# Four weight buffers, one Newton root per pair, and work moved between engines in a three-block kernel

## The chip, the cores and the metric

One Trainium2 chip, one of its cores. The metric is device time in microseconds (us) of one execution, lower is better. The chip's engines are named as in the profile: PE is TensorE (PEld its weight loads), DVE is VectorE, ACT is ScalarE, POOL is GpSimd, SP is the sync engine, which here issues all DMAs.

## What is computed

Three transformer blocks, one after the other, over one sequence of 256 tokens with 2048 channels, all in fp32.

```python
x = first_block(x, ...)    # RMS norm; w_in; RWKV-7 mixing beside banded attention,
                           # each gated by silu; two branch products, merged by sigmoid gates;
                           # w_out; x + rms_norm(o)
x = second_block(x, ...)   # RMS norm; w_in; sparse attention beside spatial gating:
                           #   vn = layer_norm(gelu(v))
                           #   mixed = einsum('gts,bcsgd->bctgd', tril(w_s), vn) + b_s
                           #   out = gelu(u) * mixed
                           # gates, w_out, squared-relu feed-forward, RMS norm
return third_block(x, ...) # pooling beside dilated attention, feed-forward, RMS norm
```

RWKV needs per head 1/max(|kk|, 1e-12) and, after its scan, 1/sqrt(var + 64e-5); every RMS norm needs 1/sqrt(mean of squares).

## The kernel before, in words

Activations lie channels on partitions: a chunk is 128 channels by 256 tokens. All large products are one stream over weights (sections `qkv` to `down3_1`, lines 196 to 218, 256 output columns per block). A unit is 1024 rows by 256 columns (1 MB), loaded by SP into `ring` (RING = 4 units). A slot is half a unit, 512 rows; there are 1084 slots. For each slot ScalarE copies the weights to their rounded high half (`split_high`, L2205) and VectorE makes the low half (`split_low`, L2212) in `w_parts` (PARTS = 3 slots). TensorE then runs eight products of 512 columns with the high half (L2282) and eight of 256 with the low half (L2288), and raises `slot_used`. When a block ends, ScalarE copies one half of the result out of PSUM (L1845), VectorE adds the other (L1932), and scaling, activation or residual follow in phases 1 to 3, some on GpSimd (L1895).

Each engine walks the slots q in the same order. In its iteration q ScalarE makes the high half of slot q + 2, and VectorE the low half. A load of unit u waits until unit u - RING is split:

```python
            if u >= RING:
                sp.wait_ge(low_split, 2 * (u - RING) + 2)
...
            if q >= PARTS:
                act.wait_ge(slot_used, q - PARTS + 1)
```

All other work runs beside the stream as threads (class `Beside`, L59): a thread has a start slot and a pace, each of its programs yields ticks, and a tick runs at place start + tick x pace, at q, q + 0.34 or q + 0.67 of that engine's walk. So the order on each engine is fixed when the kernel is built; semaphores do the rest, and a thread's step that waits holds the stream's work behind it on that engine. The start thread begins at -1 with pace 1.34.

What the change touches:

- **Start** (L306 to L444). SP loads x in two halves, then units 0 and 1. TensorE transposes x (L384), VectorE copies it out (L424) and ScalarE and VectorE split it (L409, L461). ScalarE squares whole rows after copy groups 3 and 7 (L414). VectorE makes the root, TensorE spreads it over partitions (L400), which gives `rstd`.
- **InverseRoot** (L77). A Newton root on VectorE, eleven small dependent operations (L89 to L94).
- **Rms** (L465). Squares of a block's output on ScalarE (L492, L495), added up on GpSimd into `acc` (L504) except the last, then summed over partitions on TensorE (L516): first `acc`, then the last squares, both behind the wait for the last squares.
- **Rwkv** (L812). Two threads, each four head pairs i; their side products are issued at L1026. Per i and thread VectorE copies the norm (L907), runs a root and a clamp (L911), then makes the sigmoid (L915), for which TensorE waits; and another root after the variance (L969).
- **Gates and branch.** The gates go out to `gate_scratch` in DRAM (L2001) and come back in 16 loads (L2045). The branch section has two slots a block, blocks alternating RWKV and attention, their operands split at L577 and L585 by `y_split`, then `ya_split`. Gate and branch are merged at L1954 to L1959.
- **post** (L2059 to L2110), between blocks 1 and 2 (stages out and index2): sums, root, spread, then VectorE scales o (L2071), adds x (L2075) and makes low halves (L2080); ScalarE makes high halves (L2108) and squares for `norm1`, and GpSimd adds two of those (L504).
- **Spatial gating** (L1403 to L1552), in sections ga2 and gb2. TensorE sums v over channels by 16 products with ones (L1443) and its squares by 32 (L1453). For each of 16 groups (class `Gating`, two threads, 7 ticks of 0.6 slots) TensorE transposes (L1542, L1543), ScalarE copies (L1528), VectorE masks the weights (L1516), TensorE adds the bias as a product with a row of ones (L1549) and the mixed product (L1550), and VectorE multiplies by u (L1522).

## Time and profile before

| | |
|---|---|
| median of 3 runs | 3639.61 us (3635.76 to 3640.41) |
| the profiled execution, own time | 3641.87 us |
| its span | 3640.1 us, 53150 instructions |
| PE busy | 3492.9 us (96%) |
| DVE busy | 2225.8 us (61%) |
| ACT busy | 1581.7 us (43%) |
| POOL busy | 276.9 us (8%) |
| DMA | 591.44 MB, mean 162 GB/s |
| mean granted TensorE clock | 0.977 of full |

Busy time of TensorE is the union of its matmuls; they are pipelined and their ends are modelled, so a row's duration can reach into the next one. One fp32 matmul in the code is two records in the trace outside the main stream. An idle time in brackets names what ended it. The page also has the span in 40 slices:

```profile
PEclk9999999989998999999999999999999999999999
DMA  6554332323653554544566556665545466566653
```

### The profile page before, as it was taken

The page shows a single profiled execution, that of the slowest core. Times are in us where ns is not written, and L with a number is a line of the kernel's source. Part 1 is how long each engine was busy: PE and PEld are TensorE (multiplying, and loading weights), DVE is VectorE, ACT ScalarE, POOL GpSimd, SP SyncE. Part 2 cuts the span into 40 slices and gives each one's busy share as a digit, 9 for nine tenths or more (in the row PEclk, how much of TensorE's full clock was granted, in tenths as well). Part 3 has the DMA queues.
Part 4 walks back from the last instruction along what each step waited for, and adds up shares of the span by engine and source line. Part 5 has one row for each costly group of instructions (what it writes and reads, how often), then busy time and mean ns, then how long its engine had stood idle before and what let it go on. Part 6 is the DMA issues. An engine that isn't in the chain of part 4 may idle for free.

```text
span 3640.1 us, 53150 instructions
## 1 busy us (share of the span) xinstructions
PE 3492.9 (96%) x22326; PEld 3009.5 (83%) x22326; DVE 2225.8 (61%) x3130; ACT 1581.7 (43%) x2140; POOL 276.9 (8%) x313
## 2 busy tenths in 40 slices
PE   7999999988998999999999999999999899999998
PEld 6887777767886887887888888888888788888887
DVE  5556654555746667665676546655677766456644
ACT  3444333333453445443544434444454444434444
POOL 2100122220010110000000000001000000000000
PEclk9999999989998999999999999999999999999999
DMA  6554332323653554544566556665545466566653
GB/s 187 172 176 146 116 119 91 97 90 106 219 180 88 185 174 151 174 139 139 185 183 188 185 186 184 189 193 185 175 151 161 150 187 191 188 186 186 187 183 127
DMA packets 587351, 591.44 MB, mean 162 GB/s; under 512 B 20886, under 2 KB 581350, under 8 KB 587111
## 3 DMA queue, kind: packets, MB, share of 16 engines
q1 hardware_dynamic: 587112, 588.04, 51.9%
q8 instruction: 176, 2.88, 0.3%
q14 instruction: 63, 0.52, 0.0%
HBM read 581.68 MB, written 6.32 MB: 162 GB/s over the span
## 4 chain that ended last, share of the span: by engine, by line
PE 86%; DVE 8%; ACT 3%; issue 2%; DMA 1%; SPq 0%; POOL 0%; ACTq 0%; DVEq 0%
PE gp L2282 50%; PE gp L2288 27%; PE sidep L1026 4%; DVE w_parts L2212 2%; ACT w_parts L2205 1%; PE sidep L516 1%; ACT lo_half L1845 0%; PE sidep L1549 0%; PE sidep L1550 0%; DMA high<-bias_rows 0%; DVE stage L1932 0%; DVE stage L1936 0%; DVE smalls L94 0%; DVE smalls L92 0%; PE sidep L1320 0%
## 5 line engine op out<-in xcount | busy, mean ns | idle before, releaser
L2212 DVE TENSOR_TENSOR w_parts<-ring,w_parts 128x1024 fp32r<-128x1024 f32 x1084 | 1375.0, 1277 | 917.5 <-ACT w_parts L2205 916.4
L2205 ACT ACTIVATE w_parts<-ring 128x1024 fp32r<-128x1024 f32 x1084 | 1134.2, 1056 | 1100.0 <-PE gp L2288 1040.9
L2282 PE MATMUL gp<-x_parts,w_parts 128*128 128x512 f32 x5856 | 1534.7, 402 | 28.4 <-issue 12.7
L2282 PEld LDWEIGHTS gp<-x_parts,w_parts 128*128 128x128 f32 x5856 | 1065.2, 192 | 230.9 <-issue 30.8
L2288 PEld LDWEIGHTS gp<-x_parts,w_parts 128*128 128x128 f32 x5856 | 802.3, 192 | 63.5 <-DVE w_parts L2212 5.7
L2288 PE MATMUL gp<-x_parts,w_parts 128*128 128x256 f32 x5856 | 837.5, 286 | 3.7 <-DVE w_parts L2212 3.7
L2282 PE MATMUL gp<-ff_parts,w_parts 128*128 128x512 f32 x2816 | 715.9, 396 | 4.8 <-ACT w_parts L2205 4.8
L2282 PEld LDWEIGHTS gp<-ff_parts,w_parts 128*128 128x128 f32 x2816 | 505.1, 188 | 101.8 <-ACT w_parts L2205 5.6
L2288 PEld LDWEIGHTS gp<-ff_parts,w_parts 128*128 128x128 f32 x2816 | 385.3, 188 | 32.0
L2288 PE MATMUL gp<-ff_parts,w_parts 128*128 128x256 f32 x2816 | 394.9, 282 | 0.0
L1845 ACT ACTIVATE lo_half<-gp 128x512 f32<-128x512 f32 x255 | 152.2, 597 | 479.6 <-PE gp L2288 479.4
L1932 DVE TENSOR_TENSOR stage<-gp,lo_half 128x512 f32<-128x512 f32 x184 | 127.1, 691 | 208.7 <-ACT lo_half L1845 208.6
L504 POOL TENSOR_TENSOR low<-low 128x512 f32<-128x512 f32 (+1 forms) x44 | 65.0, 1483 | 1971.6 <-ACT low L492 1319.3
L1861 ACT ACTIVATE ff_parts<-stage 128x512 fp32r<-128x512 f32 x64 | 40.5, 633 | 170.5 <-DVE stage L1967 170.5
L1026 PEld LDWEIGHTS sidep<-high 64*64 64x64 f32 x1760 | 68.4, 136 | 45.0 <-issue 18.8
L1026 PE MATMUL sidep<-high 64*64 64x64 f32 (+1 forms) x1760 | 81.9, 230 | 17.7 <-ACT high L1008 5.3
L1895 POOL TENSOR_TENSOR high<-high,rstd 128x512 f32<-128x512 f32 x40 | 56.3, 1408 | 517.0 <-DVE high L1932 517.0
L1932 DVE TENSOR_TENSOR high<-gp,lo_half 128x512 f32<-128x512 f32 x63 | 43.5, 691 | 62.2 <-ACT lo_half L1845 62.2
L1895 POOL TENSOR_TENSOR stage<-stage,rstd 128x512 f32<-128x512 f32 x32 | 43.7, 1365 | 411.3 <-DVE stage L1932 411.3
L1992 DVE TENSOR_TENSOR ff_parts<-stage,ff_parts 128x512 fp32r<-128x512 f32 x64 | 44.3, 692 | 49.1 <-ACT ff_parts L1861 49.1
L1936 DVE TENSOR_TENSOR stage<-stage,rstd 128x512 f32<-128x512 f32 x88 | 60.3, 685 | 0.2
L1967 DVE SCALAR_TENSOR_TENSOR stage<-stage 128x512 f32<-128x512 f32 x64 | 44.3, 692 | 2.2
(372 smaller groups left out, 1751.9 us busy)
## 6 DMA issues: line engine op xcount, KB each, us to landing
ring<-w_in SPq DMA_DIRECT2D x220, 1024.0 KB, 5.2
ring<-w_ff SPq DMA_DIRECT2D x128, 1024.0 KB, 5.6
ring<-w_up SPq DMA_DIRECT2D x64, 1024.0 KB, 5.8
ring<-w_down SPq DMA_DIRECT2D x64, 1024.0 KB, 5.5
ring<-w_out SPq DMA_DIRECT2D x48, 1024.0 KB, 5.5
ring<-w_branch_rwkv SPq DMA_DIRECT2D x8, 1024.0 KB, 5.5
ring<-w_branch_attn SPq DMA_DIRECT2D x8, 1024.0 KB, 5.4
gate_scratch<-stage SPq DMA_DIRECT2D x16, 256.0 KB, 2.3
```

The costliest lines, as they stand in the source:

```text
L504: m = pool.tensor_tensor(self.acc[k], self.acc[k], self.sq[b - 1][k], ALU.add)
L1026: return pe.matmul(out, lhs, rhs, start=start, stop=stop, skip_group_check=True)
L1845: act.activation(lo_half[:, k % 2], gp[:, k % 2, :, 1, :], ACT.Copy).then_inc(lo_copied, 1)
L1895: pool.tensor_tensor(to, to, over(rstd, 2), ALU.mult).then_inc(scaled_by_pool, 1)
L1932: v.tensor_tensor(to, gp[:, k % 2, :, 0, :], lo_half[:, k % 2], ALU.add).then_inc(block_evacuated, 1)
L1936: v.tensor_tensor(to, to, over(scaled_by[s.name], 2), ALU.mult).then_inc(scaled_by_vector, 1)
L1967: v.scalar_tensor_tensor(st, st, 0.0, st, ALU.max, ALU.mult).then_inc(finished_up, 1)
L1992: v.tensor_tensor(ff_parts[:, 2 * b:2 * b + 2, 1, :], st, ff_parts[:, 2 * b:2 * b + 2, 0, :].bitcast(F32), ALU.subtract).then_inc(ff_split, 1)
L2205: act.activation(w_parts[:, q % PARTS, 0], ring[:, u % RING, SLOT * (q % 2):SLOT * (q % 2) + SLOT, :], ACT.Copy).then_inc(high_split, 1)
L2212: v.tensor_tensor(w_parts[:, q % PARTS, 1], ring[:, u % RING, SLOT * (q % 2):SLOT * (q % 2) + SLOT, :], w_parts[:, q % PARTS, 0].bitcast(F ...
L2282: pe.matmul(gp[:, k % 2, j, :, :], w_parts[:, q % PARTS, 0, c, j * P:(j + 1) * P], operand(s, b, SLOT * n + c), start=(n == 0 and c == 0), ...
L2288: m = pe.matmul(gp[:, k % 2, j, 0, :], w_parts[:, q % PARTS, 1, c, j * P:(j + 1) * P], operand(s, b, SLOT * n + c)[:, 0, :], start=False, ...
```

## The change

It has these parts.

1. `w_parts` has four slots and `ring` three units. The sizes are equal, so the memory used stays the same. The order of the walks is not changed.
2. Start: unit 0 is loaded ahead of the second half of x; high and low half of slot 0 are made within the copy loop; the squares of whole rows move behind it, to tick 1 (place 0.34). The spread on TensorE moves to tick 1.25 (place 0.675), the parameter transposes to 1.5, VectorE's steps accordingly. SP loads unit 1 before the parameters and unit 2 after them, which is now all of the ring.
3. `Rms`: with three or more blocks, the `acc` half of the sums no longer waits for the last squares.
4. RWKV: thread 1 runs one root for both threads, over eight columns, after both have copied; likewise after the variance. TensorE's spreads wait for it.
5. Branch blocks alternate attention first; `ya_split` comes ahead of `y_split`, and the gate loads wait for `ya_split` as before.
6. post: the first group of four chunks is scaled and added in two halves, and its low halves come directly after; GpSimd's adds for `norm1` wait for all splits (`x_split`).
7. Gating: VectorE adds up v (two adds of 128x1024, one of their sum, one of 128x512) and the squares likewise (three of 128x1024 and one of 128x512); TensorE does 2 products instead of 16, and 4 instead of 32. The bias is loaded onto all partitions and added by VectorE before the product with u; the 32 bias products go.

The diff, cut to its core:

```diff
-RING = 4
-PARTS = 3
+RING = 3
+PARTS = 4
...
             for n in range(2):
+                if n:
+                    load_unit(sp, 0)
                 for t in range(2):
                     sp.dma_start(xrow[:, t, n * 1024:(n + 1) * 1024],
...
-            yield 1
+            yield 1.25
             pe.wait_ge(copied, 9)
             spread(pe, 1, 2, 1).then_inc(n_spread, 1)
...
-                if g in (3, 7):
-                    act.wait_ge(x_loaded[0], 32)
-                    act.wait_ge(x_loaded[1], 32)
-                    act.activation(row_squares, xrow[:, g // 4, :], ACT.Square,
-                                   accum_out=sums[:, g // 4:g // 4 + 1]).then_inc(rows_squared, 1)
+                if g == 3:
+                    split_high(act, 0)
+            yield 1
+            act.wait_ge(x_loaded[0], 32)
+            act.wait_ge(x_loaded[1], 32)
+            for t in range(2):
+                if t:
+                    act.wait_ge(rows_squared, 1)
+                act.activation(row_squares, xrow[:, t, :], ACT.Square, accum_out=sums[:, t:t + 1]).then_inc(rows_squared, 1)
...
+                if g == 4:
+                    split_low(v, 0)
-            yield 0.5
+            yield 1
             v.wait_ge(rows_squared, 2)
...
                 for part in (self.acc, self.sq[-1]):
-                    pe.wait_ge(self.squared, self.blocks)
+                    if part is not self.acc or self.blocks < 3:
+                        pe.wait_ge(self.squared, self.blocks)
...
                     dv.did(v.tensor_scalar(self.nrm, y[:, 0:4], 1e-30, None, ALU.max), "norm_copied")
-                    dv.wait(v, "norm_copied", i)
-                    dv.did(self.root.run(v, self.nrm, self.inv, self.half, self.part), "norm_rooted")
-                    dv.wait(v, "norm_rooted", i)
-                    dv.did(v.tensor_scalar(self.inv, self.inv, 1e12, None, ALU.min), "norm_inverted")
+                    if self.th == 1:
+                        for rw in rwkv:
+                            rw.dv.wait(v, "norm_copied", i)
+                        rwkv_roots.did(rwkv_root.run(v, *rwkv_eight), "norm_rooted")
+                        rwkv_roots.wait(v, "norm_rooted", i)
+                        rwkv_roots.did(v.tensor_scalar(rwkv_eight[1], rwkv_eight[1], 1e12, None, ALU.min), "norm_inverted")
...
-            sp.dma_start(bs[0:1], I["sgu_b_2"]).then_inc(sgu_loaded, 16)
+            sp.dma_start(bs, bass.AP(I["sgu_b_2"].tensor, 0, [[0, P], [P, 16], [1, P]])).then_inc(sgu_loaded, 16)
...
+            yield 4
+            pe.wait_ge(sgu_added, 4)
+            for c in range(2):
+                m = pe.matmul(sp_[:, 0, 0:TOK], ones[:, :], sgu_sq[:, 0, c, :], start=(c == 0), stop=(c == 1), skip_group_check=True)
+            m.then_inc(sgu_summed, 1)
+            yield 16
+            pe.wait_ge(sgu_added, 8)
+            for t in range(2):
+                for c in range(2):
+                    m = pe.matmul(sp_[:, 1, t:t + 1], sgu_sq[:, 0, c, t * P:(t + 1) * P], ones[:, 0:1],
+                                  start=(c == 0 and t == 0), stop=(c == 1), skip_group_check=True)
+            m.then_inc(sgu_summed2, 1)
...
-                    dv.did(v.tensor_tensor(u, self.y[:, 0:TOK], u, ALU.mult), "out")
+                    dv.did(v.tensor_tensor(self.vn.rearrange("p (t s) -> p t s", t=2), self.y[:, 0:TOK].rearrange("p (t s) -> p t s", t=2),
+                                           bs[:, g:g + 1, :].to_broadcast([P, 2, P]), ALU.add), "biased")
+                    dv.wait(v, "biased", i)
+                    dv.did(v.tensor_tensor(u, self.vn, u, ALU.mult), "out")
...
-                        pe.matmul(self.y[:, t * P:(t + 1) * P], ones[0:1, :], bs[0:1, g, :], start=True, stop=False, skip_group_check=True)
                         m = pe.matmul(self.y[:, t * P:(t + 1) * P], self.tok[:, t, :], self.tok[:, 2, :],
-                                      start=False, stop=True, skip_group_check=True)
+                                      start=True, stop=True, skip_group_check=True)
...
+        ya_split = Split(q1, 8, att_ready, S["zr"].end).thread("y_a", at("branch"))
         y_split = Split(v_, 0, y_ready, S["zr"].end).thread("y_r", at("branch"))
-        ya_split = Split(q1, 8, att_ready, S["zr"].end).thread("y_a", at("branch"))
...
-            scale(0)
-            add(0)
+            for n in range(2):
+                v.tensor_tensor(o1[:, 2 * n:2 * n + 2, :], o1[:, 2 * n:2 * n + 2, :], over(sp_[:, 1], 2), ALU.mult).then_inc(first_scaled, 1)
+                v.wait_ge(first_scaled, n + 1)
+                v.tensor_tensor(xt[:, 2 * n:2 * n + 2, :], xt[:, 2 * n:2 * n + 2, :], o1[:, 2 * n:2 * n + 2, :], ALU.add).then_inc(first_stored, 1)
+            low_halves(0)
             scale(1)
             add(1)
-            low_halves(0)
             scale(2)
...
         def post_pool(pool):
             yield 1.0
+            pool.wait_ge(x_split, norm1_xs0 + 4)
             norm1.add(pool, 1)
             norm1.add(pool, 2)
```

## Rows read from the trace of the kernel before

**Rows 1.** The page: the engine line, and one line of its DMA issues.

```profile
PE 3492.9 (96%) x22326; PEld 3009.5 (83%) x22326; DVE 2225.8 (61%) x3130; ACT 1581.7 (43%) x2140; POOL 276.9 (8%) x313
...
ring<-w_in SPq DMA_DIRECT2D x220, 1024.0 KB, 5.2
```

**Rows 2.** Stretches: stage down2_0, then ga2; busy (records), clock, DMA share, GB/s.

```profile
2029.99:2210.89 180.90, 180.90 (x1026) 157.50 (x1025) 90.13 (x82) 72.35 (x73) 0.00 (x0) 1.00 0.60 188
1524.36:1645.08 120.72, 120.72 (x709) 103.95 (x708) 73.97 (x101) 50.09 (x64) 11.19 (x8) 1.00 0.49 149
```

**Rows 3.** Groups of instructions by line: busy us, mean ns, idle before and its releaser.

```profile
L1549 PE MATMUL sidep<-high,ones 1*128 1x128 f32 x64 | 16.1, 332 | 4.7 <-DVE low L1516 4.7
...
L1443 PE MATMUL sidep<-high,ones 128*128 128x256 f32 x32 | 7.6, 379 | 0.0
...
L1453 PE MATMUL sidep<-ones,low 128*128 128x1 f32 x64 | 7.5, 246 | 0.0
...
L1478 DVE TENSOR_TENSOR high<-high,variance 128x1024 f32<-128x1024 f32 x4 | 4.9, 1220 | 0.0
```

**Rows 4.** Instructions in order of time, TensorE, in ga2: start, us, what.

```profile
1600.55 0.48 PE L1549 MATMUL sidep<-high,ones 1*128 1x128 f32 x2
1600.96 0.49 PE L1550 MATMUL sidep<-low 128*128 128x128 f32 x2
```

**Rows 5.** Order of time in the gates stage, third pair of RWKV heads; idle in brackets.

```profile
658.10 0.15 DVE L907 TENSOR_SCALAR smalls<-sidep 128x4 f32<-128x4 f32 x1
...
660.54 0.49 DVE L915 TENSOR_SCALAR high<-high 128x256 f32<-128x256 f32 x2
660.88 2.07 PE L1026 MATMUL sidep<-consts,high 128*128 128x256 f32 x4 [5.33 <-DVE high L915]
```

**Rows 6.** Waits of TensorE: whom it waited for, us in total, times, longest.

```profile
PE gp L2282 <- ACT w_parts L2205: 14.5, 6, 8.4
PE sidep L1026 <- DVE high L915: 14.0, 4, 5.3
...
PE sidep L516 <- ACT low L492: 10.2, 4, 4.1
...
PE sidep L1249 <- DVE low L1202: 5.6, 9, 1.3
...
PE sidep L1026 <- DVE smalls L94: 2.5, 2, 1.6
```

**Rows 7.** Order of time around the start of the branch stage.

```profile
898.76 3.70 PE L2282 MATMUL gp<-x_parts,w_parts 128*128 128x512 f32 x8 [6.08 <-issue]
...
902.22 8.49 SPq L2045 DMA_DIRECT2D high<-gate_scratch  x16
...
916.92 0.69 DVE L1954 SCALAR_TENSOR_TENSOR low<-high,stage 128x512 f32<-128x512 f32 x1 [7.87 <-DMA high<-gate_scratch]
...
918.81 1.66 PE L2288 MATMUL gp<-x_parts,w_parts 128*128 128x256 f32 x8 [2.37 <-DVE w_parts L2212]
```

**Rows 8.** Order of time between stages out and index2.

```profile
1086.81 3.54 PE L516 MATMUL sidep<-ones,low 128*128 128x1 f32 x16 [2.17 <-ACT low L492]
...
1102.80 5.89 DVE L2080 SCALAR_TENSOR_TENSOR x_parts<-low,prm,x_parts 128x256 fp32r<-128x256 f32 x4
...
1105.65 2.36 POOL L504 TENSOR_TENSOR high<-high 128x1024 f32<-128x1024 f32 x1 [0.52 <-ACT high L492]
...
1117.67 4.04 PE L516 MATMUL sidep<-ones,high 128*128 128x1 f32 x32
```

**Rows 9.** Order of time at the start (PEld: weight loads of TensorE).

```profile
10.42 0.71 PEld L384 LDWEIGHTS sidep<-ident,high 128*128 128x128 f32 x4 [0.20 <-DMA high<-x]
...
20.02 1.89 ACT L414 ACTIVATE high<-high 128x2048 f32<-128x2048 f32 x1
...
23.09 2.04 PE L2282 MATMUL gp<-x_parts,w_parts 128*128 128x512 f32 x4 [8.36 <-ACT w_parts L2205]
...
32.25 1.69 PEld L2282 LDWEIGHTS gp<-x_parts,w_parts 128*128 128x128 f32 x8
```

More of the change, by code:

```diff
@@ L852, in __init__ @@
                 self.nrm = smalls[:, 40 + 4 * th:44 + 4 * th]
-                self.inv, self.half, self.part = (smalls[:, 56 + 12 * th + 4 * n:60 + 12 * th + 4 * n] for n in range(3))
-                self.root = InverseRoot(sem(f"rwkv_root_{th}"))
+                self.inv = smalls[:, 56 + 4 * th:60 + 4 * th]
                 self.x, self.yk = sp_[:, 2 * th, :], sp_[:, 2 * th + 1, :]
@@ L969, in vector @@
                     dv.did(v.tensor_scalar(self.nrm, x[:, 256:260], 1.0 / 64, 64e-5, ALU.mult, ALU.add), "variance")
-                    dv.wait(v, "variance", i)
-                    dv.did(self.root.run(v, self.nrm, self.inv, self.half, self.part), "deviation_inverted")
+                    if self.th == 1:
+                        for rw in rwkv:
+                            rw.dv.wait(v, "variance", i)
+                        rwkv_roots.did(rwkv_root.run(v, *rwkv_eight), "deviation_inverted")
                     yield t0 + 68
@@ L1466, in sgu_scalar, with add @@
                 act.wait_ge(sgu_centred, g + 1)
+                if g == 0:
+                    act.wait_ge(sgu_summed, 1)
                 if g >= 2:
-                    act.wait_ge(sgu_summed2, g - 1)
-                act.activation(sgu_sq[:, g % 2], vv[:, 4 * g:4 * g + 4, :], ACT.Square).then_inc(sgu_squared, 1)
+                    act.wait_ge(sgu_added, 4 + g - 1)
+                act.activation(sgu_sq[:, min(g, 1)], vv[:, 4 * g:4 * g + 4, :], ACT.Square).then_inc(sgu_squared, 1)
         def sgu_vector(v):
+            n = 0
+            def add(to, a, b):
+                nonlocal n
+                n += 1
+                v.tensor_tensor(to, a, b, ALU.add).then_inc(sgu_added, 1)
+            yield 0.5
+            v.wait_ge(gelu_done, 8)
+            for th in range(2):
+                att2[th].dv.wait(v, "out3", 1)
+            add(sgu_sq[:, 0], vv[:, 0:4, :], vv[:, 4:8, :])
+            yield 1.5
+            add(sgu_sq[:, 1], vv[:, 8:12, :], vv[:, 12:16, :])
+            yield 2.5
+            v.wait_ge(sgu_added, 2)
+            add(sgu_sq[:, 0], sgu_sq[:, 0], sgu_sq[:, 1])
+            v.wait_ge(sgu_added, 3)
+            add(sgu_sq[:, 0, 0:2], sgu_sq[:, 0, 0:2], sgu_sq[:, 0, 2:4])
             yield 6
@@ L2105, in post_scalar @@
                 yield (0, 0, 0.34, 0.67)[g]
-                act.wait_ge(post_stored, g + 1)
+                if g:
+                    act.wait_ge(post_stored, g)
                 for c in range(4 * g, 4 * g + 4):
+                    if g == 0 and c % 2 == 0:
+                        act.wait_ge(first_stored, c // 2 + 1)
                     m = act.activation(x_parts[:, c, 0, :], xt[:, c, :], ACT.Copy, scale=par("norm1", c))
@@ L2230, in _ @@
                 side.run(-1)
-                for u in range(2):
-                    load_unit(sp, u)
+                load_unit(sp, 1)
                 side.run(-0.33)
@@ L2297, in _ @@
                 side.run(-1)
-                for q in range(2):
-                    split_high(act, q)
+                split_high(act, 1)
                 for q in range(n_slots + 1):
@@ L2321, in _ @@
                 side.run(-1)
-                for q in range(2):
-                    split_low(v, q)
+                split_low(v, 1)
                 for q in range(n_slots + 1):
```

71 lines of the change are left out of this document (34 added, 37 removed).

## The prediction, made before the change was run

> **What bounds the kernel now.** I read the page first, then the stretches by stage, then who TensorE waits for, then the order of time at each place that the diff touches. The page's engine line puts TensorE at 96% of the span and no other engine above 61% [rows 1]. A stage without side work shows what one slot costs: 64 slots take 180.90 us, 2.83 us each, TensorE busy throughout at full granted clock [rows 2]. There are 1084 slots, so 3064 us are fixed; the change touches none of them. The other 576 us are TensorE's side matmuls, its idle time and its slower clock. The page leaves only 3640.1 - 3492.9 = 147 us idle, spread over dozens of waits. A gain must be a side matmul that goes away, a wait of TensorE's that gets shorter, or clock given back.
>
> The profiled execution took 3641.87 us by its own time, over a span of 3640.1. I sum against 3641.87 and take off 2.3 us at the end, as the median of the runs is 3639.61.
>
> **Gating sums and bias (stages ga2, gb2).** In ga2, the second window of the view, TensorE is never idle [rows 2], so what it no longer does is gained. Removed: 14 of 16 sums over v (L1443), 28 of 32 sums over the squares (L1453), all 32 bias products (L1549). The groups have 7.6, 7.5 and 16.1 us busy [rows 3]. Busy counts each burst's modelled tail: a bias product shows 0.48 us for its two records, but the next matmul starts 0.41 us after it [rows 4]. So L1549 is worth 32 x 0.41 = 13.1; I scale L1443 likewise, by 0.41/0.48, and keep L1453, whose bursts are long: 6.5 x 14/16 + 7.5 x 28/32 + 13.1 = 25.4 us (upper end, unscaled: 29.3). Added on VectorE: six adds of 128x1024 at 1.22 us (nearest, L1478 [rows 3]), two half as large, and one more pass of about 0.4 us in each of 16 steps: some 15 us over the two stages. VectorE is busy 74 of 121 us in ga2 [rows 2]; that idle third hides them. If the cover fails, the cost is a wait per step: TensorE now has less between a step's transposes and its product, so the trip over ScalarE and VectorE gets tighter. I put 2 us of new waits (0 to 6). The bias load grows to 1 MB, some 3 us on SP's queue ahead of a weight unit that is wanted 15 us later: nothing. Net -23.5 (-29 to -19).
>
> **One Newton root per pair of RWKV threads.** In the order of time, thread 1's root block runs from 658.10 to 660.54, 2.44 us, after thread 0's, and TensorE stands 5.33 us for the sigmoid queued behind both [rows 5]. Of this wait 2.44 goes. It occurs four times, 14.0 us together, longest 5.3 [rows 6]: two of 5.33 and two of about 1.65, which vanish: 2 x 2.44 + 3.3 = 8.2. The second root's wait before the spread (2.5 in all, L94 [rows 6]) goes too, less 0.3 for thread 0, which now waits for the pair. Then the clock: L516 takes 3.54 us for 16 records after an idle stretch, and 4.04 for 32 where TensorE had been busy [rows 8], which is the granted clock at its two levels, 1.2 and 2.4 GHz. The product after the 5.33 us runs at the lower one (four records of 256 columns in 2.07 us [rows 5]). Some 3 us of this should come back (0 to 7). Net -13.4 (-17 to -8). Thread 0's spread now queues behind thread 1's copy, on TensorE and VectorE; as both threads' copies stand before either sigmoid already (L907 of thread 1 ahead of L915 twice [rows 5]), that costs nothing new.
>
> **Attention branch first.** TensorE idles 6.08 us before the first branch block [rows 7]. The queue of waits before it (evacuation, scale, Silu, product) stays; only the ScalarE copy for the first half operand moves ahead of the product, so 0.9 us is saved, not 6. The larger part is on SP: the 16 gate loads start at 902.22 because they wait for the attention split, now two splits earlier: some 3.2 us. VectorE waited for them until 916.92, and TensorE 2.37 us for its weights [rows 7]. That goes; but with RING = 3 the unit for slots 6 and 7 of this section stands behind those 16 loads. It lands 3 us after them, at about 916.6, where TensorE would want its split at 915.7: a new wait of 2 us. Slot 6 starts at 917.8 instead of 920.26, and the slow clock around 919 should not occur (1.1). Net -3.5 (-6 to +1).
>
> **Step between blocks 1 and 2.** The sums over squares take 3.54 us after 2.17 idle [rows 8]. The accumulated half no longer waits for the last squares, so it fills the idle time: -1.8. Half-size scale and add bring the first copies forward: -1.0. GpSimd's adds no longer run against L2080, whose four small operations took 5.89 us beside them, and TensorE's 3.7 us wait shrinks by 2. But GpSimd's two adds now start only when all splits are done, about 1111.6, and at 2.36 us each [rows 8] end at 1116.4; TensorE arrives at their consumer, L516, near 1113.7 and waits. Before it began there at 1117.67 without a wait. So of 4.8 us saved ahead, 1.3 remain. Net -1.3 (-3 to +1).
>
> The port rule of the Trainium skill (SBUF — State Buffer, section on who interferes with whom) says that GpSimd and a VectorE operation with two SBUF inputs exclude each other for a whole instruction. The trace agrees: four operations of 256 elements took 5.89 us beside L504, where one of 1024 takes 1.22. By it each of the eight gating adds could stand behind one GpSimd operation; at 2.36 us each that is 19 us, and the sum would lose up to that.
>
> **Sums of the other norms.** L516 waits four times for the last squares, 10.2 us, longest 4.1 [rows 6]; 2.17 of it is the step above. At the norm after out3a and at the final one the idle time is longer than half the sums, so half of about 3.5 us goes, 1.8 each; a short gap gives 0.5, and one of another kind (L495) 0.8. Net -4.9 (-6.5 to -3).
>
> **Start.** The squares leave the copying loop, unit 0 is loaded before the second half of x, and slot 0 is split early. x's second half was waited for at 10.42 [rows 9]. A MB takes some 3 us: the gates' 4 MB took 14.7 from first issue to use (902.22 to 916.92 [rows 7]), 2 of them latency. The 1 MB unit ahead of x thus delays it to 13.4. TensorE starts slot 0 near 15.6 instead of 23.09, 7.5 us earlier. But the squares (1.89 each, [rows 9]) now come after the third high split, end at 27.5, the root at 30.0, and the spread, moved by its tick to 0.675, stands ahead of slot 1. Slot 1 then starts near 30.9 instead of 32.25 [rows 9], at the low clock after 11 us idle, which costs 2 to 3. The 17 parameter loads stay on SP, ahead of unit 2, as before. Net +1 (-1 to +3).
>
> **Four weight buffers.** PARTS = 4 lets ScalarE split a slot earlier wherever slot_used held it back. It helps only where TensorE waits for VectorE or ScalarE work queued behind a split; the program order, look-ahead q + 2, is unchanged, and each block's end still waits for TensorE. Of the waits I count as candidates L1249 (5.6), L2282 outside the start (14.5 - 8.4 = 6) [rows 6], and some 15 us of small ones below them. The out3a waits in L2282 are a ping-pong of ScalarE and VectorE that no buffer shortens. I take 8 (0 to 20), a third. RING = 3 costs nothing outside the branch: a unit lands 5.2 us after issue [rows 1] and is wanted two units, 11.3 us, later.
>
> **Sum.** -23.5 - 13.4 - 3.5 - 1.3 - 4.9 + 1 - 8 = -53.6: 3588.3, and **3586 us** against the median.
>
> **Rivals.**
> *The moved work comes back.* VectorE's added passes and its exclusion by GpSimd delay each of the 16 gating steps by about 1 us, and the fourth buffer is inert, because the order and not the buffer was the limit. For: TensorE already waits on VectorE at L1549 (4.7 us [rows 3]), and the look-ahead is not changed, so in this part the change may not do what it says. Against: the idle third of VectorE. 3586 + 16 + 8 = 3610. This is also how the port rule of the Trainium skill (SBUF — State Buffer) would act.
> *More comes back.* Buffers worth 20, clock 4 more: 3586 - 12 - 4 = 3570. For: each idle stretch near 3 us is often followed by the low clock. Against: most waits are round trips.
> *Three load buffers starve the splits.* A ring buffer is held for its landing, 5.2, and while its two slots are split, 5.65; with three the pace is 10.85 / 3 = 3.6 us per unit, against 5.65 wanted. It decides where landing exceeds 11.3 us; at 12 every unit would come after 5.88, and 542 x 0.23 = 125 us are lost: 3711, slower than before. For: three buffers are the fewest that could hide a late one, and the gates' loads take 14.7 us. Against: 5.2 us is the median over 220 such loads [rows 1].
>
> **Chances.** Forecast 0.62, moved work back 0.20, more back 0.15, starved 0.02, other 0.01. The range must hold 0.8: from 3566 to 3612, which takes in the first two rivals and the bounds of the terms. 0.2% (7 us) is what a measurement of this kernel can tell; all cases but the last two lie far below: faster 0.96, same 0.02, slower 0.02.
>
> **What would show it.** Gone: L1549's group; L1443 at 4 records and L1453 at 8; the second root block per pair. TensorE's wait for L915 near 5 to 6 us instead of 14.0. First matmul of slot 0 near 15.6, then a long wait for the root. The gate loads near 3 us earlier against the branch's start, and a wait for L2205 at its seventh slot. A new wait at L516 for GpSimd after index2 begins. ga2 at 97 to 101 us instead of 120.7. Wrong would be: ga2 above 108 us, TensorE waits that grow by more than 10 us in all, or ring landings above 8 us.

## Result: 3591.6 us, and the profile after

The changed kernel took 3591.59 us (median; 3589.37 to 3595.99), the kernel before 3637.69 in the same comparison: ratio 0.987, 95% interval 0.9858 to 0.9883. That is 1.3% less time. The forecast of 3586 us is 5.6 us too low and the time lies inside the range.

Page of the kernel after, engine line, granted clock in 40 slices, and the ring's loads (they answer to [rows 1]):

```profile
PE 3445.4 (96%) x22178; PEld 2978.3 (83%) x22178; DVE 2208.9 (62%) x3064; ACT 1553.7 (43%) x2140; POOL 279.7 (8%) x313
PEclk9999999999999999999999999999999999999999
...
ring<-w_in SPq DMA_DIRECT2D x220, 1024.0 KB, 5.3
```

TensorE's busy time fell by 3492.9 - 3445.4 = 47.5 us. Its idle time hardly fell: 3590.2 - 3445.4 = 144.8 us, against 147.2. So waits that went were replaced by waits that came, and nearly all of the gain is matmuls that are gone and matmuls that run at a higher clock: the mean granted clock of the span is 0.983, before 0.977.

Where the time went, by stage: stretches of the kernel after; us, busy of TensorE (records), its weight loads, VectorE, ScalarE, GpSimd; clock, DMA share, GB/s.

```profile
0.00:183.11 183.11, 163.34 (x889) 141.78 (x889) 99.30 (x113) 73.43 (x92) 35.26 (x75) 0.97 0.57 179
412.78:791.26 378.48, 346.77 (x4167) 288.16 (x4165) 208.66 (x402) 128.98 (x246) 93.02 (x90) 0.97 0.32 104
791.26:872.96 81.70, 73.04 (x863) 60.27 (x861) 41.79 (x77) 28.91 (x47) 5.21 (x6) 1.00 0.29 91
872.96:966.77 93.81, 91.38 (x512) 79.76 (x513) 68.02 (x75) 43.74 (x52) 0.00 (x0) 0.98 0.71 224
966.77:1069.67 102.90, 93.67 (x534) 81.54 (x533) 53.45 (x65) 51.95 (x71) 10.91 (x6) 0.96 0.55 174
1069.67:1123.45 53.78, 45.91 (x228) 40.29 (x229) 36.60 (x80) 20.88 (x29) 6.73 (x2) 0.83 0.32 85
1496.59:1611.29 114.70, 103.93 (x592) 90.50 (x591) 83.50 (x117) 50.03 (x64) 12.06 (x8) 0.96 0.54 164
1611.29:1714.56 103.27, 98.56 (x564) 86.37 (x563) 74.60 (x94) 45.14 (x58) 10.37 (x8) 0.97 0.52 161
```

In order these are the start with qkv, gates, zr, branch, out, index2, ga2 and gb2. The same stages of the kernel before:

```profile
0.00:185.41 185.41, 165.04 (x888) 141.93 (x889) 99.33 (x113) 74.96 (x92) 35.09 (x75) 0.95 0.57 180
416.53:811.96 395.43, 355.90 (x4167) 294.29 (x4165) 219.15 (x483) 131.37 (x246) 93.41 (x90) 0.94 0.31 100
811.96:898.76 86.80, 76.92 (x862) 63.50 (x861) 43.74 (x88) 29.58 (x47) 5.22 (x6) 0.93 0.27 86
898.76:994.04 95.28, 92.91 (x512) 81.10 (x513) 68.55 (x75) 45.13 (x52) 0.00 (x0) 0.96 0.69 221
994.04:1100.59 106.55, 95.37 (x534) 83.16 (x533) 56.31 (x65) 54.20 (x75) 10.91 (x6) 0.93 0.54 164
1100.59:1149.04 48.45, 44.74 (x228) 39.34 (x229) 35.20 (x78) 19.83 (x26) 5.67 (x2) 0.83 0.36 100
...
1645.08:1757.76 112.68, 107.98 (x597) 91.21 (x596) 72.54 (x86) 46.72 (x58) 10.36 (x8) 0.97 0.49 150
```

Gates and zr together give 22.0 us, the two gating stages 15.4 (ga2 was 120.72 [rows 2]), the start 2.3, branch 1.5, out 3.6; index2 lost 5.3. In the gates stage TensorE has the same 4167 records and is busy 9.1 us less: that is the clock, 0.94 to 0.97. Its idle time there fell too, from 39.5 to 31.7 us. The remaining 10 us are spread over stages that are not shown here, with 3.2 in qkv2, 2.9 in in3, 2.5 in down3_1 and 1.5 in rkv as the largest.

Whom TensorE waited for in the kernel after (us in total, times, longest); it answers to [rows 6]:

```profile
PE sidep L402 <- DVE smalls L94: 13.5, 3, 10.1
...
PE sidep L1041 <- DVE high L928: 10.2, 3, 5.0
PE gp L2331 <- ACT w_parts L2255: 7.2, 6, 1.4
...
PE sidep L525 <- ACT low L500: 6.5, 3, 3.2
...
PE sidep L1462 <- DVE low L1488: 5.6, 1, 5.6
...
PE sidep L525 <- POOL high L512: 4.5, 1, 4.5
PE sidep L1456 <- DVE low L1488: 3.4, 1, 3.4
```

The waits for ScalarE's splits (L2255, L2205 before) read 7.2 us instead of 14.5, but 8.4 of the 14.5 was the first slot of the kernel [rows 9]. Without it they rose, from 6.1 to 7.2. The norm sums wait less for the last squares (L525, L516 before), 6.5 us instead of 10.2. L928 is the sigmoid, L915 before: 10.2 us, where 14.0 stood and 5 to 6 were forecast. The others are new: L402 waits 10.1 us for the root at the start, as forecast; L1462 and L1456, the two sums of the gating norm, wait 9.0 us for VectorE's adds (L1488); L525 waits 4.5 us for GpSimd's adds in index2.

### The profile page after: what moved, and what is told of

Same layout as the page of the kernel before. It is cut to its first block, busy times and chain, and to the rows that moved or that the text cites. A ratio compares the mean times of both kernels' runs of the same rounds, so it can differ in the third digit from the quotient of the medians.

```text
span 3590.2 us, 52791 instructions
## 1 busy us (share of the span) xinstructions
PE 3445.4 (96%) x22178; PEld 2978.3 (83%) x22178; DVE 2208.9 (62%) x3064; ACT 1553.7 (43%) x2140; POOL 279.7 (8%) x313
## 4 chain that ended last, share of the span: by engine, by line
PE 87%; DVE 7%; ACT 3%; issue 2%; DMA 1%; POOL 0%; ACTq 0%; SPq 0%; DVEq 0%; POOLq 0%
PE gp L2331 51%; PE gp L2337 27%; PE sidep L1041 4%; DVE w_parts L2262 2%; ACT w_parts L2255 1%; PE sidep L525 0%; ACT lo_half L1889 0%; DVE stage L1976 0%; DVE stage L1980 0%; DMA ring<-w_branch_rwkv 0%; PE sidep L1594 0%; PE sidep L1258 0%; DVE high L1976 0%; PE sidep L1264 0%; DVE low L1488 0%
## 5 line engine op out<-in xcount | busy, mean ns | idle before, releaser
L2255 ACT ACTIVATE w_parts<-ring 128x1024 fp32r<-128x1024 f32 x1084 | 1110.9, 1052 | 449.4 <-PE gp L2337 356.4
```

The costliest lines, as they stand in the source:

```text
L2255: act.activation(w_parts[:, q % PARTS, 0], ring[:, u % RING, SLOT * (q % 2):SLOT * (q % 2) + SLOT, :], ACT.Copy).then_inc(high_split, 1)
```

## The experiments

Seven kernels take one part of the change back, four edit one place of it, and one puts three edits together. All stand against the kernel before; the kernel after is 0.9870, and 0.0010 is 3.6 us. The intervals are 0.0013 to 0.0023 wide to each side, 5 to 8 us, so small effects are read from the stage's own row of the profile. Such a row is one execution, and the last section tells how far it moves by itself.

**The root of both threads.**

```diff
-                    if self.th == 1:
-                        for rw in rwkv:
-                            rw.dv.wait(v, "norm_copied", i)
-                        rwkv_roots.did(rwkv_root.run(v, *rwkv_eight), "norm_rooted")
+                    dv.wait(v, "norm_copied", i)
+                    dv.did(self.root.run(v, self.nrm, self.inv, self.half, self.part), "norm_rooted")
```

> The kernel after, with a Newton root for each RWKV thread again, nothing else undone. The stages gates and zr took 460.2 us after and 482.2 before, 22.0 less, where 13.4 was forecast. Theory: the root alone does it. TensorE's waits in these stages (49.4 us of idle before, 40.4 after) come back by 8 to 10 us, and the granted clock of the two stages (0.94 and 0.93 before, 0.97 and 1.00 after) falls back, so that 15 to 22 us return: 3607 to 3614 us, gates + zr 475 to 482. Rival: part of the 22 belongs to the fourth weight buffer, which lets the splits run ahead of the RWKV work; then only 8 to 13 return: 3600 to 3605, gates + zr 468 to 473.

Measured: 3602.38 us, ratio 0.9900 (0.9886 to 0.9913), 0.0030 above the kernel after, 11 us. Stages gates and zr:

```profile
411.64:802.41 390.77, 352.98 (x4166) 292.38 (x4164) 220.70 (x483) 129.07 (x246) 94.00 (x90) 0.95 0.31 100
802.42:884.16 81.74, 73.07 (x864) 60.26 (x861) 43.35 (x88) 28.93 (x47) 5.22 (x6) 1.00 0.29 91
```

Gates is 12.3 us longer, zr unchanged: 472.5 together. The longer stage is half idle time (37.8 us instead of 31.7) and half clock (busy 353.0 instead of 346.8). The wait for the sigmoid is back in four places, the longest of 7.2 us:

```profile
PE sidep L1035 <- DVE high L924: 13.6, 4, 7.2
```

The root is worth 11 to 12 us, in the gates stage alone, and the rival's numbers hold. The 5.1 us that zr gained do not come from the root.

**Four split buffers, three load buffers.**

```diff
-RING = 3
-PARTS = 4
+RING = 4
+PARTS = 3
```

> The kernel after, with four load buffers and three split buffers again. Theory: the fourth split buffer is worth what the waits for the splits lost, 18.2 us before (14.5 and 3.7) and 9.9 after (7.2 and 2.7), so 4 to 8 us, spread over branch, out3a and the like: 3596 to 3600 us, gates + zr unchanged at 460. Rival one: it also carries part of the RWKV stages' gain; then 12 to 18: 3604 to 3610, gates + zr 468 to 475. Rival two: what the split buffer gives, the load buffer takes; 3589 to 3594 and ring landings no longer than now.

Measured: 3601.51 us, ratio 0.9896 (0.9882 to 0.9909): 0.0026, 9.5 us, just above the theory's size. Gates took 379.63 us, 1.2 more, so rival one falls for that stage. The loss comes in small amounts from five stages: qkv 2.2, rkv 2.7, zr 2.6, qkv2 3.2, ga2 2.9. Each has a lower granted clock, and some 4.6 of these 13.7 us are idle time. In zr and ga2 such differences come and go by themselves (last section). The theory's reason does not hold, though its size does, because the main stream's waits for the splits did not come back:

```profile
PE gp L2331 <- ACT w_parts L2255: 6.2, 5, 1.4
```

They are 7.2 us in the kernel after. Branch gained 1.4 us and has no idle time of TensorE at all. That fits four load buffers which reach past the gate loads, but several kernels with three took 92.6 to 93.4 us too.

**The gating norm's sums back on TensorE.**

```diff
-            yield 4
-            pe.wait_ge(sgu_added, 4)
-            for c in range(2):
-                m = pe.matmul(sp_[:, 0, 0:TOK], ones[:, :], sgu_sq[:, 0, c, :], ...
+            yield 1
+            pe.wait_ge(gelu_done, 8)
...
+            for c in range(DC):
+                m = pe.matmul(sp_[:, 0, 0:TOK], ones[:, :], vv[:, c, :], ...
```

> The kernel after, with the gating norm's sums on TensorE as before; the bias stays on VectorE. Theory: the two waits that stand in ga2 now, 3.4 us at the sum over v and 5.6 us at the sum over the squares, both for the adds on VectorE, and the two half-clock stretches behind them (6.8 and 3.4 us, worth 5.1) take what the removed matmuls give (6.5 x 14/16 + 7.5 x 28/32 = 12.3 us). Then undoing it costs nothing: 3588 to 3594 us, ga2 112 to 116 us with clock 1.00 and no idle time. Rival: the idle time is of VectorE's other work and stays whoever sums; then 12 us are lost: 3600 to 3606, ga2 near 125.

Measured: 3592.32 us, ratio 0.9870 (0.9855 to 0.9886), the same as with the sums on VectorE. Stage ga2:

```profile
1496.83:1610.27 113.44, 111.64 (x677) 98.74 (x675) 76.12 (x109) 49.91 (x64) 11.25 (x8) 1.00 0.54 166
```

TensorE is idle 1.8 us here and 10.8 with the change, and its clock is 1.00 instead of 0.96. The 85 records more cancel against the shorter waits and the better clock: this part of the change gave nothing that these runs can tell. Seven kernels with the ga2 of the kernel after took 113.2 to 116.3 us for it.

**The bias products back on TensorE.**

```diff
+                        pe.matmul(self.y[:, t * P:(t + 1) * P], ones[0:1, :], bs[0:1, g, :], start=True, stop=False, skip_group_check=True)
                         m = pe.matmul(self.y[:, t * P:(t + 1) * P], self.tok[:, t, :], self.tok[:, 2, :],
-                                      start=True, stop=True, skip_group_check=True)
+                                      start=False, stop=True, skip_group_check=True)
```

> The kernel after, with the 32 bias products back on TensorE and the short bias load; the sums stay on VectorE. Theory: they cost 0.41 us each, 13.1 us, and nothing is given back for them: 3603 to 3606 us, ga2 + gb2 231 us instead of 218. Rival: the trip over VectorE got longer by the added pass, so that part of the 13.1 became waits for the next step's data (TensorE waits 6.5 us for the scaled value now, 4.7 before); then 6 to 10: 3597 to 3602.

Measured: 3615.02 us, ratio 0.9934 (0.9921 to 0.9946): 0.0064, 23 us. Both theory and rival were too small. Stages ga2 and gb2:

```profile
1496.99:1618.64 121.65, 112.70 (x625) 95.57 (x623) 80.60 (x109) 50.03 (x64) 12.04 (x8) 0.96 0.49 150
1618.64:1738.41 119.77, 115.07 (x597) 96.51 (x596) 71.67 (x86) 45.14 (x58) 10.38 (x8) 0.90 0.44 135
```

They are 7.0 and 16.5 us longer. Why more than 13.1 shows in the order of time, one gating step of the kernel before and one of the kernel after:

```profile
1601.38 0.48 PE L1549 MATMUL sidep<-high,ones 1*128 1x128 f32 x2
1601.79 0.49 PE L1550 MATMUL sidep<-low 128*128 128x128 f32 x2
```

```profile
1599.31 0.65 PE L1594 MATMUL sidep<-low 128*128 128x128 f32 x4
```

Before, a step was four such groups at about 0.42 us, from 1600.55 [rows 4] to 1602.28: 1.73 us. Now its product is one burst of 0.65. What goes is 1.08 us a step and, if all steps are like this one, 17.3 over 16: the product matmuls that stood between bias products were themselves slower. Eight steps lie in each stage, 8.6 us. In ga2 1.8 us less idle time stands against them. In gb2 the other 7.9 us are the lower clock, 0.90 against 0.97, and they are not the bias products' own: the kernel before has the same 597 records and the same 4.7 us of idle time there and took 112.68 us at 0.97. So the 23 us of this run overstate what the bias products cost.

**The step between blocks 1 and 2.** Old orders on VectorE, ScalarE's waits with them, and:

```diff
         def post_pool(pool):
             yield 1.0
-            pool.wait_ge(x_split, norm1_xs0 + 4)
             norm1.add(pool, 1)
             norm1.add(pool, 2)
```

> The kernel after, with the step between blocks 1 and 2 as before: both orders on VectorE, and no wait of GpSimd for the low halves; the relaxed wait at the start of a norm's sums stays. The stages out, index2 and qkv2 took 307.6 us after and 309.2 before. Theory: the step's own part is near zero, since what the earlier split gives ahead of index2 (3.6 us in out's end) comes back as the wait for GpSimd's adds (4.5 us at the norm's sums) with a half-clock stretch behind it (3.4 us long, worth 1.7): undoing gives 3589 to 3593 us. Rival one, the forecast: 1.3 us gained, so 3592 to 3594. Rival two: the GpSimd wait costs more than all the rest, index2 and qkv2 get shorter by 5 or more when it goes: 3583 to 3587.

Measured: 3588.85 us, ratio 0.9865 (0.9846 to 0.9883). That is no clear difference to 0.9870, but the stages are clear; out and index2:

```profile
969.37:1073.34 103.97, 93.67 (x535) 81.58 (x533) 55.51 (x65) 53.24 (x75) 10.90 (x6) 0.96 0.54 172
1073.34:1120.22 46.88, 43.38 (x229) 37.88 (x229) 34.92 (x78) 19.49 (x26) 5.64 (x2) 0.88 0.37 98
```

With the old step out is 1.1 us longer and index2 6.9 shorter. Over the ten kernels with the new step and GpSimd's adds, index2 took 51.5 to 54.3 us. So the new step costs some 5 us here, as in rival two, though the whole time lies next to the theory's. Kernel after, at this place, GpSimd and then TensorE:

```profile
1082.71 6.87 POOL L512 TENSOR_TENSOR high<-high 128x1024 f32<-128x1024 f32 x2 [32.64 <-DVE x_parts L2124]
```

```profile
1089.64 6.99 PE L525 MATMUL sidep<-ones,high 128*128 128x1 f32 x32 [4.54 <-POOL high L512]
```

The two adds begin only when the low halves are done and take 3.4 us each while VectorE works, not 2.36 as forecast. TensorE waits 4.54 us and then runs its 32 sums at the lower clock (granted 0.50 throughout), 6.99 us where they took 4.04 [rows 8].

**The adds on VectorE**, with the new order kept:

```diff
             yield 0.67
             low_halves(3)
+            yield 1.0
+            norm1.add(v, 1)
+            norm1.add(v, 2)
```

> The kernel after, with the two adds of the first norm of block 2 taken from GpSimd (where they start at 1082.7, behind the low halves, and take 6.9 us) and given to VectorE, one weight slot into index2; the new order of the step stays. Theory: the late adds are what makes the new step cost more than it gives (index2 53.8 us, but 46.9 with the old step); TensorE's wait of 4.5 us for them goes, with a half-clock stretch: index2 46 to 48, out 102.9, 3582 to 3587 us. Rival: it is the 2.4 us of adds on VectorE ahead of a split, or the lower clock of this stage in any case (0.83), that keeps index2 above 50: 3588 to 3591.

Measured: 3591.55 us, ratio 0.9866 (0.9847 to 0.9885). Index2, and qkv2 behind it:

```profile
1071.93:1117.33 45.40, 42.32 (x228) 36.74 (x229) 35.25 (x82) 20.88 (x29) 0.00 (x0) 0.91 0.39 101
1117.33:1272.63 155.30, 150.87 (x804) 127.34 (x803) 98.33 (x135) 55.37 (x60) 19.05 (x14) 0.96 0.53 164
```

```profile
1088.73 3.63 PE L525 MATMUL sidep<-ones,high 128*128 128x1 f32 x32
```

The local theory holds: no wait, the 32 sums in 3.63 us, index2 8.4 us shorter. The forecast of the whole time, 3582 to 3587, fails: qkv2, with the same instructions and the same idle time, took 155.30 us instead of 150.91, zr 84.4 instead of 81.7, ga2 115.5 instead of 114.7. The four executions spread from 3586.26 to 3600.14 us, so this median says little of an edit worth 8. The section on the hardware comes back to this.

**The start as before.** Unit 0 after all of x, squares in the copy loop, first splits behind the start:

```diff
             for n in range(2):
-                if n:
-                    load_unit(sp, 0)
                 for t in range(2):
```

> The kernel after, with the start as before. The first 48 slots ended at 183.1 us after and 185.4 before. Theory: all of that is the start, so undoing costs 2.3 us: 3593 to 3595, with the end of qkv at 185.4. Rival: the fourth split buffer gave it and the start itself lost 1 us as forecast: 3589 to 3591, the end of qkv near 182.

Measured: 3598.68 us, ratio 0.9890 (0.9872 to 0.9908), 7 us above the kernel after, with an interval as wide. Qkv ends at 185.2 us instead of 183.1, as the theory had it. The rest lies above all in zr (84.4 us) and qkv2 (155.3), where nothing was edited and only the clock differs, so 2 us is what this run shows of the start. Undoing only the buffers put that end at 185.3 too: the two parts give these 2 us together and neither alone. The section on the prediction shows where they come from.

**The attention branch second again.**

```diff
-            w = (I["w_branch_attn"], I["w_branch_rwkv"])[b % 2][0]
+            w = (I["w_branch_rwkv"], I["w_branch_attn"])[b % 2][0]
...
+        y_split = Split(v_, 0, y_ready, S["zr"].end).thread("y_r", at("branch"))
         ya_split = Split(q1, 8, att_ready, S["zr"].end).thread("y_a", at("branch"))
-        y_split = Split(v_, 0, y_ready, S["zr"].end).thread("y_r", at("branch"))
```

> The kernel after, with the rwkv branch ahead of the attention branch again. The stage branch took 93.8 us after and 95.3 before; its start has one wait of 5.05 us, 6.6 before. Theory: undoing brings that back, with 1 to 3 us, and the rest of the time does not move: 3592 to 3595, branch 95 to 97. Rival: with three load buffers the gates' reload, which waits for nothing of the branch order, meets the splits either way; then the order is worth nothing and branch stays at 92 to 94.

Measured: 3598.08 us, ratio 0.9879 (0.9864 to 0.9893), 0.0009 above the kernel after, 3 us; branch 97.03 us, 3.2 more, its first wait 6.08 us instead of 5.05. The theory holds in its stage. Of the 3.2 us 0.7 is idle time and the rest clock (0.95 for 0.98); in the other eleven changed kernels branch took 92.4 to 94.9.

**Can the two waits of ga2 go?** First by time alone (adds two slots earlier, second sum, root and spread one slot later):

```diff
-            yield 0.5
+            yield -3.5
             v.wait_ge(gelu_done, 8)
...
-            yield 16
+            yield 18
             pe.wait_ge(sgu_added, 8)
```

> The kernel after, with the gating norm's adds over v two blocks' halves (two weight slots) earlier on VectorE, and with TensorE's sum over the squares, the root and its spread one slot later. Theory: both waits for the adds in ga2 go (3.4 and 5.6 us) with the half-clock stretches behind them (worth 5.1 us), and nothing takes their place, since the first gating step starts a slot after the spread: 3577 to 3581 us, ga2 100 to 103. Rival: VectorE is late in ga2 for its own queue, so the second sum waits 2 to 4 us all the same, or the first gating step is late for its root: 3583 to 3587.

Measured: 3588.30 us, ratio 0.9862 (0.9843 to 0.9881), ga2 109.19 us. The first wait went, the second stayed at 4.56 us though its sum came a slot later. ScalarE shows why, in the same kernel:

```profile
1530.21 1.06 ACT L1480 ACTIVATE low<-high 128x1024 f32<-128x1024 f32 x1 [4.37 <-DVE low L1488]
1531.18 1.04 ACT L2255 ACTIVATE w_parts<-ring 128x1024 fp32r<-128x1024 f32 x1
```

The last square needs the buffer that VectorE's add must free. The square stands 4.37 us on ScalarE, the split (L2255) queues behind it, and VectorE's last adds queue behind that split. So a third buffer, on top of the same times:

```diff
+        sgu_third = low[:, 6144:7168].rearrange("p (c t) -> p c t", c=4)
+        squares_of = (sgu_sq[:, 0], sgu_sq[:, 1], sgu_third, sgu_sq[:, 1])
...
-                if g >= 2:
-                    act.wait_ge(sgu_added, 4 + g - 1)
+                if g == 3:
+                    act.wait_ge(sgu_added, 5)
```

> The gating norm's adds timed as in sums_timed, and a third buffer for its squares, so that ScalarE's third and fourth squares wait for no add. In sums_timed the wait before the sum over the squares stayed at 4.6 us. Theory: that wait is a round trip: the fourth square stood on ScalarE for 4.4 us (with a split queued behind it) until VectorE had added the square before it. Without the trip the sums over the squares find their adds done: no wait for L1488 in ga2, ga2 99 to 103 us at clock 1.00, 3580 to 3585 us. Rival: VectorE is simply behind at this place, waiting for block ends; then the wait stays at 3 us or more and ga2 at 107 to 110.

Measured: 3582.04 us, ratio 0.9837 (0.9822 to 0.9851). Stage ga2, and its second sum (busy, mean ns, idle before):

```profile
1493.99:1597.94 103.95, 99.94 (x593) 87.31 (x592) 82.98 (x117) 50.05 (x64) 17.54 (x8) 1.00 0.59 181
```

```profile
L1464 PE MATMUL sidep<-ones,low 128*128 128x1 f32 x8 | 1.1, 253 | 0.5 <-DVE low L1490 0.5
```

The round trip was the cause. The wait is 0.5 us instead of the 4.56 of sums_timed, the clock 1.00, and ga2 10.7 us shorter than in the kernel after. Against the sums on TensorE (113.44) it is 9.5 us, where 12.3 were forecast. A wait of 1.7 us for the root remains.

**The sigmoid ahead of the common root.**

```diff
                     dv.did(v.tensor_scalar(self.nrm, y[:, 0:4], 1e-30, None, ALU.max), "norm_copied")
+                    ac.wait(v, "decay", i)
+                    sg = self.sg.rearrange("p t c -> p (t c)")
+                    dv.did(v.tensor_scalar(sg, sg, 0.5, 0.5, ALU.mult, ALU.add), "sigmoid")
                     if self.th == 1:
```

> The kernel after, with each RWKV thread's sigmoid pass moved ahead of the common root on VectorE. TensorE waits 10.2 us in three places for that pass now, since the chain of the root (some 3.9 us beside GpSimd's multiplication) and a split stand ahead of it. Theory: these waits fall to under 2 us and the half-clock stretches behind two of them go; the spread of the root then waits up to 1 us longer per pair: 3578 to 3584 us. Rival: the root's spread is due right behind, so TensorE waits there instead and the time moves under 3 us: 3589 to 3592.

The place in the kernel after:

```profile
753.27 1.18 DVE L92 TENSOR_TENSOR smalls<-smalls 128x8 f32<-128x8 f32 x1
...
756.17 1.22 DVE L2262 TENSOR_TENSOR w_parts<-ring,w_parts 128x1024 fp32r<-128x1024 f32 x1
757.30 0.49 DVE L928 TENSOR_SCALAR high<-high 128x256 f32<-128x256 f32 x2
...
757.65 2.08 PE L1041 MATMUL sidep<-consts,high 128*128 128x256 f32 x4 [5.01 <-DVE high L928]
```

One operation of the root's chain took 1.18 us, where its like take 0.17, while GpSimd multiplied a 128x512 block from 753.17 to 754.43. Then comes a split, and only then the sigmoid.

Measured: 3586.27 us, ratio 0.9859 (0.9840 to 0.9877). Stage gates, and the same place:

```profile
412.37:783.31 370.94, 344.04 (x4167) 286.91 (x4165) 209.30 (x402) 129.03 (x246) 93.20 (x90) 0.98 0.32 106
```

```profile
747.51 1.13 PE L1040 MATMUL sidep<-consts,high 128*128 128x256 f32 x4
...
751.69 0.66 PE L1040 MATMUL sidep<-ident,smalls 128*64 128x128 f32 x8 [3.04 <-DVE smalls L927]
```

Gates is 7.5 us shorter. The wait for the sigmoid is gone; the spread waits 3.0 us for the root now, more than the 1 us that the theory allowed, but with a product done before it. The whole time, 4 us less, lies between the theory (3578 to 3584) and the rival (3589 to 3592).

**Three of these together** (third buffer with its times, sigmoid first, adds on VectorE).

> Three edits on the kernel after together: the third buffer and earlier adds of the gating norm, the sigmoid ahead of the common root, and the two adds of the first norm of block 2 on VectorE. Alone they stood at 0.9837, 0.9859 and 0.9866 of before, against 0.9870. Theory: they lie in different stages and add up, 12.0 + 4.0 + 1.5 us: 3572 to 3576 us, gates 371, index2 45 to 47, ga2 104, with a few us either way by where the half-clock stretches fall. Rival: the gains in waits are given back in clock in the stages behind them, as index2's 8 us were in adds_vector: then 3579 to 3583.

Measured: 3569.30 us (3567.21 to 3570.84), ratio 0.9810 (0.9787 to 0.9833), the fastest of all: 66.6 us under the kernel before, some 22 under the change. Ga2 took 103.9 us, gates 370.9, index2 48.2, qkv2 150.9. The edits add up, and somewhat more came than the 3572 to 3576 of the theory. Qkv2 is back at 150.9 with the adds on VectorE, so they do not by themselves bring the 155.3 of adds_vector.

## Why the prediction was right, and where it was not

The time came out right because the matmuls of the gating do go and the root is on the path. Of the forecast gain of 53.6 us 46.1 came. Part of this is luck. The range is 46 us wide and takes in two rivals, and errors of single terms cancel in part: the gating part gave 8 us less than forecast and the step 6, the start 3 more and the buffers some 1.5. The seven parts undone one at a time add up to some 52 us by their whole times, each uncertain by 5 us or more. Step by step:

- *Gating sums and bias*, forecast -23.5, measured -15.4 over ga2 and gb2. Two sizes were off. The bias products cost 17.3, not 32 x 0.41 = 13.1: the step "a bias product shows 0.48 us, but the next matmul starts 0.41 after it" counted only their own slots, not the slower product matmuls beside them. The step "I put 2 us of new waits (0 to 6)" failed: 9.0 us of waits at the two sums, and the clock at 0.96, worth up to 0.045 x 115 = 5 us. The account nearly closes: 17.3 and the sums' 12.3, less 10.8 us of idle time in ga2 and 4 to 5 of clock, leave 14 to 15. I had argued from VectorE's idle third. That share says that the adds fit, not that they are done when the sum is due; a buffer freed by VectorE held ScalarE, and so the splits (third_buffer shows it). The mark "ga2 at 97 to 101, wrong above 108" was missed at 114.7.
- *The root*, forecast -13.4, measured -11 to -12. The waits did not vanish as I had it: of the 10.4 us (8.2 and 2.2) the idle time of gates shows 6.1 with the root alone. L915 was to fall to 5 or 6 us and fell to 10.2: one place of 5.01 remained because the one chain, slowed by GpSimd, and a split still stand ahead of the sigmoid. More came as clock than my 3 us: of the 9.1 us that the gates stage is busy less for the same records, 353.0 - 346.8 = 6.2 go with the root alone. What gates and zr gained beyond the root and the buffers' 1.2 and 2.6, some 6 us of 22, no part brought back; its cause stays open. The 2.6 in zr is no sure gain of the buffers either, since six kernels that keep them took 84.4 us there too.
- *The branch order*, forecast -3.5, measured -3.2 in its stage. The first wait fell by 1.03 us (0.9 forecast). The gate loads start 2.3 us earlier in the stage, not 3.2, and VectorE has its data 17.0 us into it (889.99 - 872.96) instead of 18.2, so TensorE's wait for it shrank from 2.37 to 1.41 us and did not vanish. The new wait for L2255 at the seventh slot came, 1.0 us for 2.
- *The step*, forecast -1.3, measured about +5 in its stages, and +2 with the interval around zero in the time: the sign was wrong. The wait at L525 was foreseen, at 2.7 us (1116.4 less 1113.7; with all the 4.8 us saved ahead TensorE would come at 1112.9, a wait of 3.5); it was 4.5, since the adds take 3.4 us each beside VectorE, and the sums behind it ran at the lower clock, 3 us more. I priced the wait and not the clock behind it.
- *The other norms*, forecast -4.9. Not run alone. The stages with such sums fell by 2.9, 0.4, 1.0 and 2.5 us (in3, out3p, up3_0, down3_1), beside part of out's 3.6, and their idle time by 0.8, 0.4, 0.9 and 0.8; that fits but shows no cause. In in3 the kernels with this edit took 210.2 or 211.9 us with the same idle time.
- *The start*, forecast +1, measured -2.3, together with the buffers. The order of time was as put: slot 0 at 15.64 us (15.6 forecast), the root's spread at 28.92 after a wait of 10.1. Slot 1 started at 29.76, 1.1 us before the forecast. "At the low clock after 11 us idle, which costs 2 to 3" was paid in part, and hidden by something else. The stretch from 29.7 to 35.0, in the kernels before, after and undo_bufs:

```profile
29.70:35.00 5.30, 5.30 (x29) 4.76 (x28) 0.85 (x1) 1.06 (x1) 0.00 (x0) 0.80 1.10 250
29.70:35.00 5.30, 5.30 (x24) 4.47 (x24) 5.23 (x10) 0.25 (x1) 0.00 (x0) 0.69 0.48 143
29.70:35.00 5.30, 5.30 (x20) 4.42 (x20) 2.33 (x3) 0.00 (x0) 0.00 (x0) 0.55 0.98 246
```

Slot 1 took 4.73 us in the kernel after, 5.40 in undo_bufs and 2.89 before. From its start to the end of qkv it was 153.4, 155.6 and 153.1 us. So undo_bufs paid some 2.5 us. In the kernel after 1.8 us were paid in slot 1 and came back later: between 88 and 98 us its clock is 1.00, where before, undo_bufs and undo_start show 0.83 for the same idle time. What the buffers have to do with that stretch is not shown.

- *Four weight buffers*, forecast -8, measured -9.5 (interval some 5 us to each side). The size came out, the mechanism did not. The waits that I counted hardly moved: L1249 (L1264 after) from 5.6 to 5.1 us, the main stream's for ScalarE outside the start from 6.1 up to 7.2. What undo_bufs lost is clock for the most part, in other stages.
- *The rivals.* The moved work came back in part, by the two waits, not by 1 us a step: the product's waits for the masked weights (L1558, L1516 before) went from 4.7 to 6.5 us over both stages. The buffers are not inert. Nothing starved: ring loads land in 5.3 to 6.1 us by their medians. The port rule of the Trainium skill (SBUF — State Buffer, section on who interferes with whom) has its effect here, at another place than the gating: GpSimd's adds took 3.4 us each beside VectorE in index2, and VectorE's four small operations, 5.89 us before [rows 8] and 5.87 in undo_step, took 1.67 us in the kernel after, where GpSimd stood still. Of the eight gating adds none took more than 1.22 us, so the 19 us of that rival did not come.

## What to carry to other kernels

When work moves from the bound engine to one with idle time, look for the round trip: which buffer must the new operation free, who waits for it, and what is queued behind that waiter. Here a third buffer and earlier adds were worth 12 us by the whole time and 10.7 in their stage, on a part that had brought nothing. Put what another engine waits for ahead of a long chain on the same queue, and price a wait together with the matmuls behind it.

## What was not expected of the hardware

The granted clock moves a stage by several microseconds where nothing was edited. Stage qkv2 has the same instructions in all kernels with four split buffers, and TensorE's idle time in it is 4.4 us in each. It took 150.7 to 151.0 us at clock 0.99 in nine of them and 155.3 at 0.96 in three (undo_start, sums_timed, adds_vector). In the kernel after, to be held against the row of adds_vector:

```profile
1123.45:1274.36 150.91, 146.49 (x804) 124.51 (x803) 98.32 (x135) 55.36 (x60) 19.02 (x14) 0.99 0.53 169
```

Zr took 81.7 or 84.4 us in the same way, idle 8.7 in both, ga2 113.2 to 116.3 with 10.8 idle, and gb2 with the bias products 112.7 or 119.8 with 4.7 idle (before, undo_bias). So a stage can give back 3 to 7 us that an edit elsewhere saved, and adds_vector met two such places. Where idle time and records of a stage agree, a difference of this size in one execution does not show an effect of the edit. What decides which way a stage falls was not settled.

The other is the price of two alternating small matmuls: with the bias product between them, the 128-column products went from 0.65 us for four to 0.42 us for each pair, at the same clock. Why is not shown.
